# First and last branch product of the merges: high and low halves of u side by side in 512 columns

## The chip, the cores and the metric

The kernel runs on one core of one Trainium2 chip. The metric is the time of one execution on the device, in microseconds (us), as the median of three runs. Everything is fp32 in and out. A profiled execution of the kernel before, recorded by the hardware profiler, is what all rows below come from.

Engines are named as the profile names them: PE is TensorE's matmuls, PEld its weight loads, DVE is VectorE, ACT is ScalarE, POOL is GpSimd, SP is SyncE (it issues the weight DMAs).

## The reference

A transformer of two ordinary layers (attention or retention, then an MLP) followed by one "hybrid" layer, over 256 tokens and a model width of 1024. The change lies in the last step but one of the hybrid layer. Cut to that:

```
ya = (moba_attention(...)  * silu(mg)) @ w_up_moba     # 256x512 @ 512x1024
yb = (dsa_attention(...)   * silu(dg)) @ w_up_dsa
yc = (cross_attention(...) * silu(xg)) @ w_up_cross
gates = sigmoid(glog + b_merge)                        # glog = h @ w_in, 3 x 1024 columns
u = gates[0] * ya + gates[1] * yb + gates[2] * yc
out = rmsnorm(x + u @ w_out)
```

So there are three merges i = 0, 1, 2 (moba, dsa, cross), and each adds gate times branch product into u.

## The kernel before, in words

Every product is made to fp32 precision out of three fp32r products. A weight is split into a high and a low part (`whi` by ACT at L1047, `wlo` = raw - whi by DVE at L1558), and so is the activation; high x high, high x low and low x high are added in PSUM. Weights arrive in halves of 128x1024 elements, numbered in one long order. ACT splits up to 5 halves ahead of the half in use, DVE 4.

A product with transposed output (128 output features by 256 tokens) can be laid out in two ways:

- **Narrow**, `t_half`: three matmuls of 256 columns for each 128 rows of depth (L445, L446, L447). Two output blocks share one PSUM bank of 512 columns, and the result is complete in PSUM. DVE's one `scalar_tensor_tensor` (L2151) reads it there.
- **Wide**, `u_block`: the high and the low activation stand side by side as 512 columns. One matmul of 512 columns multiplies them by the high weight (L521), and one of 256 columns adds the low weight times the high activation to the left half (L530). Each output block takes a whole bank, whose halves have to be added afterwards: ACT copies the right half to SBUF (`branch_low`, L1232), DVE adds the left half to it (L2140), and only then the `scalar_tensor_tensor` runs, from SBUF (L2147).

Each merge i works in two groups g = 0, 1 of 512 features, so a product is named (i, g). A group is six steps on PE: four halves of gate weights "gl" (wide everywhere, `t_block`, L500 and L509), then two halves of the branch's weights "wu". Before the change the products (0, 1), (1, 0), (1, 1) and (2, 0) are wide and (0, 0) and (2, 1) are narrow. Each engine has its own program with the same steps in the same order; between the steps of merge 0 lies the attention "D" (transposes at L680, their evacuation by ACT at L1151 and by DVE at L1705), so that DVE's and ACT's programs reach a step when their own queues get there.

PSUM has eight banks, handed out by a ring in the PE program:

```
b = ring.popleft()                  # take
if b in held:
    w.wait_ge(*at("free", held[b])) # PE waits until the last user's result is read
...
ring.append(bank_of[name])          # give, at the end of the product
```

A bank is thus reused eight takes later or so, and the wait is on whatever instruction frees the product that had it: for a narrow branch product the L2151 that reads it, for a wide one the L2140 that reads that block. Only the *first* instruction of a new product waits, but everything behind it on PE waits too, since an engine runs its instructions in order.

After the last product, (2, 1), PE multiplies u by w_out ("w2o", L572), eight halves of weights. The first four need u of group 0 only. The last four are one piece: `t = [weights(...) for x in range(4)]` waits for all four weight halves, and for u of group 1, before its first matmul. On DVE the order there is: splits of earlier halves, `branch(2, 1)`, `u_low(1)` (L2207; it follows ACT's `u_high(1)`, L1516), then the low parts of w2o's halves 3 to 7 (L1558).

Of the kernel before, what the change touches and what calls it, by code (L numbers as in the profile page):

```python
# [50 lines left out]
XK, XV = 17408, 18432  # L51
EO, ED, EB = 16656, 16784, 17040
SP = 257
WIDE_UP = ((0, 1), (1, 0), (1, 1), (2, 0))
WIDE = ((0, 0), (0, 1), (1, 0), (1, 1), (2, 0), (2, 1))


# [94 lines left out]
def program(nc, A, out):  # L152
    with ExitStack() as st:
# [28 lines left out]
        def up(sem, *events):  # L182

            count[sem] = count.get(sem, 0) + 1
            for name in events:
                value[name] = (S[sem], count[sem])
            return S[sem], 1

        def at(*event):

            return value[event] if rehearsed else value.get(event, (None, 0))
# [24 lines left out]
        def bank(*name):  # L216
            return psum[bank_of.get(name, 0)][:, :]
# [142 lines left out]
        def x_split(stage, k):  # L360

            return ("xl", stage, k)
# [60 lines left out]
        def pe_program(e):  # L423
# [49 lines left out]
            def t_half(label, j, n, nk, xT, splits):  # L473

                i = first_half[label] + j
                h, l = weights(i)
                for c in range(n // 256):
                    m = j * (n // 256) + c
                    if m % 2 == 0:
                        take("mm", label, m // 2)  # L480
                    o = bank("mm", label, m // 2)[:, (m % 2) * 256:(m % 2) * 256 + 256]
                    for k in range(nk):
                        w.wait_ge(*at(*splits(k)))
                        mm = mm3(o, (h[:, k, c * 128:c * 128 + 128], l[:, k, c * 128:c * 128 + 128]),
                                 (xT[0][:, k, :], xT[1][:, k, :]), k == 0, k == nk - 1)
                    if m % 2:
                        mm.then_inc(*up("mm", ("mm", label, m // 2), ("wd", i)))
                        give("mm", label, m // 2)
                    elif c == n // 256 - 1:
                        mm.then_inc(*up("wd", ("wd", i)))  # L490
# [477 lines left out]
            def merge_half(i, s):  # L968
# [5 lines left out]
                elif r < 4:  # L974
                    t_half(("gl", i, g, r // 2), r % 2, 256, 8, hT, lambda k: x_split("sec", k))
                elif (i, g) in WIDE_UP:
                    label, j = ("wu", i, g), r - 4
# [50 lines left out]
        def act_program(e):  # L1028
# [21 lines left out]
            def used(label, j):  # L1050
                weights_to(first_half[label] + j + HI_AHEAD)
# [174 lines left out]
            def branch_low(i, g):  # L1226

                for m in range(4):
                    w.wait_ge(*at("mm", ("wu", i, g), m))
                    if (i, g) != WIDE_UP[0]:  # L1230
                        w.wait_ge(*at("ub", *WIDE_UP[WIDE_UP.index((i, g)) - 1], m // 2))
                    e.activation(UL[:, m, :], bank("mm", ("wu", i, g), m)[:, 256:512], ACT.Copy).then_inc(*up("aev", ("uc", i, g, m)))  # L1232
# [205 lines left out]
            def merge_half(i, s):  # L1438
# [6 lines left out]
                else:  # L1445
                    if r == 2:
                        gate(i, g, 0)
                    if r == 4:
                        gate(i, g, 1)
                if s == 6 and (i, 0) in WIDE_UP:  # L1450
                    branch_low(i, 0)
                used(("gl", i, g, r // 2) if r < 4 else ("wu", i, g), r % 2)
                if s == 11 and (i, 1) in WIDE_UP:
                    branch_low(i, 1)
# [10 lines left out]
            def gate(i, g, c):  # L1465
                w.wait_ge(*at("tt", i, g, c))
                for m in range(2):
                    k = 4 * g + 2 * c + m
                    d = tT[:, 2 * c + m, :]
                    w.wait_ge(*at("hb"))  # L1470
                    a = e.activation(d, d, ACT.Tanh, bias=hb[:, 8 * i + k:8 * i + k + 1], scale=0.5)
                a.then_inc(*up("aev", ("th", i, g, c)))
# [65 lines left out]
        def dve_program(e):  # L1538
# [597 lines left out]
            def branch(i, g):  # L2136
                wide = (i, g) in WIDE_UP
                for m in range(4 if wide else 0):
                    w.wait_ge(*at("uc", i, g, m))
                    e.tensor_tensor(UL[:, m, :], bank("mm", ("wu", i, g), m)[:, 0:256], UL[:, m, :], ALU.add).then_inc(  # L2140
                        *up("dev", ("ua", i, g, m), ("free", ("mm", ("wu", i, g), m))))
                for n in range(2):
                    t, d = tT[:, 2 * n:2 * n + 2, :], uT[:, 4 * g + 2 * n:4 * g + 2 * n + 2, :]
                    w.wait_ge(*at("th", i, g, 1))
                    if wide:
                        w.wait_ge(*at("ua", i, g, 2 * n + 1))
                        x = e.scalar_tensor_tensor(t if i else d, t, 1.0, UL[:, 2 * n:2 * n + 2, :], ALU.add, ALU.mult)  # L2147
                        x.then_inc(*up("dev", ("ub", i, g, n), ("u", i, g)))
                    else:
                        w.wait_ge(*at("mm", ("wu", i, g), n))  # L2150
                        x = e.scalar_tensor_tensor(t if i else d, t, 1.0, two(bank("mm", ("wu", i, g), n)), ALU.add, ALU.mult)  # L2151
                        x.then_inc(*up("dev", ("ub", i, g, n), ("u", i, g), ("free", ("mm", ("wu", i, g), n))))
                    if i:
                        w.wait_ge(*at("ub", i, g, n))
                        e.tensor_tensor(d, d, t, ALU.add).then_inc(*up("dst", ("u", i, g)))
# [307 lines left out]
```

## Time and profile before

| | |
|---|---|
| median of 3 runs | 972.54 us (971.98 to 972.82) |
| the profiled execution | 971.9 us |
| its span in the trace | 970.1 us |
| PE busy | 962.4 us, 99% of the span |
| DVE busy | 705.1 us, 73% |
| ACT busy | 554.9 us, 57% |
| weight and input DMA | 174.72 MB, 180 GB/s on average |

Times in rows are microseconds from the start of the span. A busy PE is one on which a matmul is in flight; matmuls overlap in the records, so the distance between two starts, and not the duration of one, is what a matmul costs in a stream.

### The profile page before, as it was taken

How to read it: one execution, taken by the hardware profiler on the slowest of the kernel's cores; microseconds unless marked ns; L12 is line 12 of the kernel's file. 1: busy time of each engine (PE TensorE's matmuls, PEld its weight loads, DVE VectorE, ACT ScalarE, POOL GpSimd, SP SyncE). 2: the span in 40 equal slices, each digit the busy share in tenths (PEclk: the TensorE clock that was granted, in tenths of full speed). 3: DMA queues.
4: the chain of work that ended last, by engine and by line, in shares of the span. 5: the costliest groups of instructions: out<-in, count | busy, mean ns of one | idle time of the engine just before them, and what ended most of it. 6: DMA issues, size and time to landing. Idle time of an engine off the chain costs nothing.

```text
span 970.1 us, 13894 instructions
## 1 busy us (share of the span) xinstructions
PE 962.4 (99%) x5288; PEld 825.5 (85%) x5288; DVE 705.1 (73%) x1093; ACT 554.9 (57%) x957; POOL 154.3 (16%) x189
## 2 busy tenths in 40 slices
PE   9999999999999999999999999999999999999997
PEld 8888888888888888888888888888888888988885
DVE  6888676766666767786667556666758989888884
ACT  6688655445556553455456444544535857866662
POOL 2741018920001002220001000000550110000000
PEclk9999999999999999999999999999999999999999
DMA  9984535565564664345555665555544563553631
GB/s 343 304 246 169 175 130 193 191 222 176 177 206 149 214 210 133 130 141 204 177 171 184 206 211 180 174 192 182 206 152 150 152 196 112 170 155 131 216 131 44
DMA packets 110338, 174.72 MB, mean 180 GB/s; under 512 B 4288, under 2 KB 73024, under 8 KB 110272
## 3 DMA queue, kind: packets, MB, share of 16 engines
q1 hardware_dynamic: 109840, 173.40, 54.1%
q8 instruction: 42, 0.69, 0.3%
q10 hardware_dynamic: 432, 0.44, 0.1%
q14 instruction: 24, 0.20, 0.1%
HBM read 172.78 MB, written 1.05 MB: 179 GB/s over the span
## 4 chain that ended last, share of the span: by engine, by line
PE 99%; issue 1%; DVE 0%; POOLq 0%; POOL 0%; DVEq 0%
PE ps L572 24%; PE ps L542 14%; PE ps L445 9%; PE ps L447 9%; PE ps L446 9%; PE ps L500 9%; PE ps L546 7%; PE ps L509 5%; PE ps L521 2%; PE ps L668 1%; PE ps L680 1%; PE ps L700 1%; PE ps L530 1%; PE ps L624 1%; PE ps L772 0%
## 5 line engine op out<-in xcount | busy, mean ns | idle before, releaser
L1558 DVE TENSOR_TENSOR wlo<-raw,whi 128x1024 fp32r<-128x1024 f32 x312 | 374.2, 1238 | 13.7 <-PE ps L572 8.3
L1047 ACT ACTIVATE whi<-raw 128x1024 fp32r<-128x1024 f32 x312 | 315.8, 1049 | 34.4 <-PE ps L572 22.0
L572 PE MATMUL ps<-whi,ur 128*128 128x512 f32 x656 | 182.0, 390 | 0.0
L572 PEld LDWEIGHTS ps<-whi,ur 128*128 128x128 f32 x656 | 121.1, 188 | 23.5
L542 PE MATMUL ps<-hT,whi 128*128 128x512 f32 x592 | 140.5, 389 | 0.0
L542 PEld LDWEIGHTS ps<-hT,whi 128*128 128x128 f32 x592 | 110.7, 188 | 22.8
L445 PE MATMUL ps<-whi,hT 128*128 128x512 f32 (+1 forms) x312 | 122.0, 391 | 0.0
L447 PE MATMUL ps<-whi,hT 128*128 128x512 f32 (+1 forms) x312 | 120.0, 385 | 0.0
L446 PE MATMUL ps<-wlo,hT 128*128 128x512 f32 (+1 forms) x312 | 119.9, 384 | 0.0
L1928 DVE TENSOR_TENSOR arena<-ps,arena 128x256 f32<-128x256 f32 x80 | 33.4, 423 | 98.6 <-ACT arena L1290 98.6
L1290 ACT ACTIVATE arena<-ps 128x256 f32<-128x256 f32 x80 | 30.1, 384 | 127.3 <-PE ps L546 127.3
L572 PE MATMUL ps<-wlo,ur 128*128 128x512 f32 x328 | 101.5, 390 | 0.0
L500 PE MATMUL ps<-hT,whi 128*128 128x512 f32 x368 | 97.8, 396 | 0.0
L546 PEld LDWEIGHTS ps<-hT,wlo 128*128 128x128 f32 x592 | 75.9, 191 | 2.9
L546 PE MATMUL ps<-hT,wlo 128*128 128x256 f32 x592 | 76.8, 283 | 0.0
L500 PEld LDWEIGHTS ps<-hT,whi 128*128 128x128 f32 x368 | 66.0, 189 | 12.1 <-issue 0.8
L572 PEld LDWEIGHTS ps<-wlo,ur 128*128 128x128 f32 x328 | 61.6, 188 | 13.2
L447 PEld LDWEIGHTS ps<-whi,hT 128*128 128x128 f32 x312 | 58.6, 188 | 11.8
L445 PEld LDWEIGHTS ps<-whi,hT 128*128 128x128 f32 x312 | 58.7, 188 | 11.6 <-issue 1.0
L446 PEld LDWEIGHTS ps<-wlo,hT 128*128 128x128 f32 x312 | 58.7, 188 | 10.6
L2250 POOL TENSOR_SCALAR stat<-stat 128x1 f32<-128x1 f32 x10 | 1.9, 191 | 335.0 <-ACT arena L1056 334.9
L509 PEld LDWEIGHTS ps<-hT,wlo 128*128 128x128 f32 x368 | 50.9, 190 | 4.2
(232 smaller groups left out, 1284.0 us busy)
## 6 DMA issues: line engine op xcount, KB each, us to landing
raw<-in_w SPq DMA_DIRECT2D x64, 1024.0 KB, 5.6
raw<-in_w_in SPq DMA_DIRECT2D x34, 1024.0 KB, 5.2
raw<-in_w_in_o SPq DMA_DIRECT2D x24, 1024.0 KB, 5.2
raw<-in_w_out_o SPq DMA_DIRECT2D x8, 1024.0 KB, 4.9
raw<-in_w_in_e SPq DMA_DIRECT2D x5, 1024.0 KB, 12.6
raw<-in_w_mem SPq DMA_DIRECT2D x4, 1024.0 KB, 10.2
raw<-in_w_out_e SPq DMA_DIRECT2D x4, 1024.0 KB, 5.0
raw<-in_w_out SPq DMA_DIRECT2D x4, 1024.0 KB, 5.0
```

Source lines behind the costliest of these rows:

```text
L445: e.matmul(o, a[0], b[0], start=start, stop=False)
L446: e.matmul(o, a[0], b[1], start=False, stop=False)
L447: return e.matmul(o, a[1], b[0], start=False, stop=stop)
L500: return e.matmul(o, h[:, k, :], hTs[:, k * 512:k * 512 + 512], start=k == 0, stop=k == 7)
L509: e.matmul(o[:, 0:256], l[:, k, :], hT[0][:, k, :], start=False, stop=False)
L542: e.matmul(o[m], hl[m][0][:, k, :], hTs[:, k * 512:k * 512 + 512], start=k == 0, stop=False)
L546: mm = e.matmul(o[m][:, 0:256], hl[m][1][:, k, :], hT[0][:, k, :], start=False, stop=k == 7)
L572: mm = e.matmul(bank("acc", stage, 2 * tb + i), x[p], t[p % 2][:, 0, 512 * i:512 * i + 512], start=start and p == 0, stop=stop and p == 2)
L1047: e.activation(split_half(i)[0], raw_half(i), ACT.Copy).then_inc(*up("hi", ("hi", i)))
L1290: e.activation(dst, bank("mm", label, m)[:, 256:512], ACT.Copy).then_inc(*up("aev", ("lc", label, m)))
L1558: e.tensor_tensor(l, raw_half(i), h.bitcast(F32), ALU.subtract).then_inc(*up("lo", ("lo", i)))
L1928: e.tensor_tensor(d, bank("mm", label, m)[:, 0:256], d, ALU.add).then_inc(*up("dev", ("t", label, m), ("free", ("mm", label, m))))
```

## The change

The tuple that says which branch products are wide gets (0, 0) and (2, 1) as well, so that all six are.

```diff
-WIDE_UP = ((0, 1), (1, 0), (1, 1), (2, 0))
+WIDE_UP = ((0, 0), (0, 1), (1, 0), (1, 1), (2, 0), (2, 1))
```

Three programs read it. On PE, `merge_half` calls `u_block` instead of `t_half`:

```python
elif (i, g) in WIDE_UP:
    label, j = ("wu", i, g), r - 4
    for c in range(2):
        u_block(label, first_half[label] + j, 2 * j + c, c, 4, ...)
else:
    t_half(("wu", i, g), r - 4, 512, 4, ur[i % 2], ...)
```

On ACT, `branch_low(0, 0)` and `branch_low(2, 1)` are added; on DVE, `branch` adds halves first and reads SBUF after.

TensorE's program around product (0, 0), from its second half of weights to the start of gate product gl (0, 1). Before (L445 to L447 are the narrow product, L680 the transposes of attention D, L500 the gate product's first matmuls):

```order
2448 L445 MATMUL ps<-ur,whi 128x256
2449 L446 MATMUL ps<-ur,whi 128x256
2450 L447 MATMUL ps<-ur,wlo 128x256
2451 L680 MATMUL ps<-cst,arena 128x128 [waits s_aev]
2452 L680 MATMUL ps<-cst,arena 128x128 x3
2453 L680 MATMUL ps<-cst,arena 128x128 [waits s_aev]
2454 L680 MATMUL ps<-cst,arena 128x128 x3
2455 L500 MATMUL ps<-hT,whi 128x512 [waits s_hi,s_dev]
```

The same place after the change; s_dev is the semaphore that DVE raises when it has read a bank:

```order
2415 L521 MATMUL ps<-ur,whi 128x512 x4
2416 L530 MATMUL ps<-ur,wlo 128x256 x4
2417 L521 MATMUL ps<-ur,whi 128x512
2418 L680 MATMUL ps<-cst,arena 128x128 [waits s_aev,s_dev]
2419 L680 MATMUL ps<-cst,arena 128x128 x3
2420 L680 MATMUL ps<-cst,arena 128x128 [waits s_aev,s_dev]
2421 L680 MATMUL ps<-cst,arena 128x128 x3
2422 L500 MATMUL ps<-hT,whi 128x512 [waits s_hi,s_dev]
```

The row L500 waits for s_dev in both, but for another instruction. The ring's takes, one after the other, were before: wu (0,0) bank 0 of 2; two for transposes D; wu (0,0) bank 1 of 2; two for transposes D; gl (0,1). The gate product then got the bank of the gate product gl (0,0) block 2, which L2123 frees. Now the takes are: wu (0,0) blocks 0 and 1; two for transposes; blocks 2 and 3; two for transposes; gl (0,1). That is eight takes after block 0 of wu (0,0), so the gate product gets its bank, which the first L2140 of `branch(0, 0)` frees.

VectorE's program around `branch(0, 0)` (L1705 is the evacuation of the last transposes D, L2123 that of gate product gl (0, 1)):

```order
 L1705 COPY arena<-ps 128x512
-L2151 SCALAR_TENSOR_TENSOR arena<-arena,ps 128x512 x2
+L2140 TENSOR_TENSOR arena<-ps,arena 128x256 x4
+L2147 SCALAR_TENSOR_TENSOR arena<-arena 128x512 x2
 L1558 TENSOR_TENSOR wlo<-raw,whi 128x1024 x2
 L2123 TENSOR_TENSOR arena<-ps,arena 128x256 x2
```

Nothing is moved; four additions are put in front of the two instructions that read the product, and those read SBUF.

VectorE's program around `branch(2, 1)`, in front of w2o's last splits:

```order
 L1558 TENSOR_TENSOR wlo<-raw,whi 128x1024 x2
-L2151 SCALAR_TENSOR_TENSOR arena<-arena,ps 128x512
-L2155 TENSOR_TENSOR arena<-arena 128x512
-L2151 SCALAR_TENSOR_TENSOR arena<-arena,ps 128x512
+L2140 TENSOR_TENSOR arena<-ps,arena 128x256 x4
+L2147 SCALAR_TENSOR_TENSOR arena<-arena 128x512
+L2155 TENSOR_TENSOR arena<-arena 128x512
+L2147 SCALAR_TENSOR_TENSOR arena<-arena 128x512
 L2155 TENSOR_TENSOR arena<-arena 128x512
 L2207 SCALAR_TENSOR_TENSOR ur<-arena,ur 128x512 x2
```

Here the four additions stand ahead of both pairs; before, the first pair stood ahead of the product's end.

## Rows read from the trace of the kernel before

**Rows 1.** The page, part 1: busy time, share, instructions of each engine.

```profile
PE 962.4 (99%) x5288; PEld 825.5 (85%) x5288; DVE 705.1 (73%) x1093; ACT 554.9 (57%) x957; POOL 154.3 (16%) x189
```

**Rows 2.** Waits of TensorE, whole span: all there is (total, times, longest).

```profile
PE ps L772 <- DVE arena L1868: 1.2, 1, 1.2
```

**Rows 3.** Timeline, PE, narrow product (2, 1): start, us, instruction, shapes, count.

```profile
935.88 0.28 PE L445 MATMUL ps<-ur,whi 128*128 128x256 f32 x1
...
941.52 0.28 PE L447 MATMUL ps<-ur,wlo 128*128 128x256 f32 x1
941.64 0.63 PE L572 MATMUL ps<-whi,ur 128*128 128x512 f32 x2
```

**Rows 4.** Timeline, PE, wide product (2, 0), first and last matmuls, and what follows.

```profile
919.09 0.86 PE L521 MATMUL ps<-ur,whi 128*128 128x512 f32 x3
...
924.47 0.40 PE L521 MATMUL ps<-ur,whi 128*128 128x512 f32 x1
924.71 1.77 PE L500 MATMUL ps<-hT,whi 128*128 128x512 f32 x7
```

**Rows 5.** Timeline, PE, behind product (0, 0): transposes D, then gl (0, 1).

```profile
835.10 1.03 PE L680 MATMUL ps<-cst,arena 128*128 128x128 f32 x8
835.89 1.86 PE L500 MATMUL ps<-hT,whi 128*128 128x512 f32 x7
```

**Rows 6.** Timeline, DVE, up to branch (0, 0); brackets: idle before, and releaser.

```profile
834.00 0.76 DVE L2123 TENSOR_TENSOR arena<-ps,arena 128x256 f32<-128x256 f32 x2 [3.69 <-ACT arena L1462]
...
838.07 1.22 DVE L1558 TENSOR_TENSOR wlo<-raw,whi 128x1024 fp32r<-128x1024 f32 x1
839.20 0.68 DVE L1705 COPY arena<-ps 128x512 f32<-128x512 f32 x1
839.80 1.27 DVE L2151 SCALAR_TENSOR_TENSOR arena<-arena,ps 128x512 f32<-128x512 f32 x2
```

**Rows 7.** Timeline, ACT, where branch_low(0, 0) comes in (between these two).

```profile
837.28 0.57 ACT L1151 ACTIVATE arena<-ps 128x512 f32<-128x512 f32 x1
837.76 1.99 ACT L1047 ACTIVATE whi<-raw 128x1024 fp32r<-128x1024 f32 x2
```

**Rows 8.** The page, part 5: TensorE's weight loads for a gate product (last: idle).

```profile
L500 PEld LDWEIGHTS ps<-hT,whi 128*128 128x128 f32 x368 | 66.0, 189 | 12.1 <-issue 0.8
```

**Rows 9.** Timeline, ACT and DVE behind the wide product (2, 0).

```profile
924.90 0.39 ACT L1232 ACTIVATE arena<-ps 128x256 f32<-128x256 f32 x1 [1.02 <-PE ps L521]
...
925.32 0.42 DVE L2140 TENSOR_TENSOR arena<-ps,arena 128x256 f32<-128x256 f32 x1 [0.98 <-ACT arena L1232]
925.66 0.68 DVE L2147 SCALAR_TENSOR_TENSOR arena<-arena 128x512 f32<-128x512 f32 x1
...
927.71 0.69 DVE L2155 TENSOR_TENSOR arena<-arena 128x512 f32<-128x512 f32 x1
...
928.43 1.16 ACT L1516 ACTIVATE ur<-arena 128x512 fp32r<-128x512 f32 x2 [2.20 <-DVE arena L2155]
```

**Rows 10.** Timeline, ACT and DVE behind the narrow product (2, 1).

```profile
943.28 1.16 ACT L1516 ACTIVATE ur<-arena 128x512 fp32r<-128x512 f32 x2 [3.74 <-DVE arena L2155]
943.95 1.29 DVE L2207 SCALAR_TENSOR_TENSOR ur<-arena,ur 128x512 fp32r<-128x512 f32 x2 [0.70 <-ACT ur L1516]
...
945.16 4.63 DVE L1558 TENSOR_TENSOR wlo<-raw,whi 128x1024 fp32r<-128x1024 f32 x4
...
950.10 1.23 DVE L1558 TENSOR_TENSOR wlo<-raw,whi 128x1024 fp32r<-128x1024 f32 x1 [0.31 <-PE ps L572]
```

**Rows 11.** Timeline, PE: inside w2o's last piece, and the last matmul.

```profile
953.00 0.62 PE L572 MATMUL ps<-wlo,ur 128*128 128x512 f32 x2
...
963.20 0.39 PE L572 MATMUL ps<-whi,ur 128*128 128x512 f32 x1
```

**Rows 12.** Windows: length; PE, PEld, DVE, ACT, POOL busy (count); granted clock, DMA.

```profile
968.20:968.60 0.40, 0.00 (x0) 0.00 (x0) 0.00 (x0) 0.00 (x0) 0.00 (x0) 0.82 1.02 389
```

## Prediction, written before the changed kernel ran

> **What bounds the kernel now.** I read the page first: PE has a matmul in flight in 962.4 of 970.1 us [rows 1]. The waits of TensorE say the same more sharply: in the whole span it waited once, for 1.2 us, at the very start [rows 2]. So TensorE is the bound from end to end, and two things follow. Whatever makes its stream shorter shows in the time at once. And whatever makes it wait, for even one microsecond, shows in the time too, and can't be made good later, since there is no later wait that could shrink; after the last matmul only the normalisation and the output follow, some 6.5 us from 963.59 to 970.1, which the change doesn't touch. The questions are what the wide form saves on TensorE, and whether the longer evacuation makes it wait.
>
> **What the wide form saves.** For one branch product TensorE has 48 matmuls of 256 columns before, and 16 of 512 plus 16 of 256 after: 12,288 columns both times. The trace has both forms. The narrow (2, 1) begins at 935.88 and the next work begins at 941.64: 5.76 us [rows 3]. The wide (2, 0) begins at 919.09 and the next begins at 924.71: 5.62 us [rows 4]. So a product gets shorter by 0.14 us, both together by 0.28 us. That is 0.03% of the time; what a measurement of this kernel can tell from no change is about 0.2%, or 1.9 us.
>
> **Product (0, 0): a bank that comes free late.** This is the term that decides. Before, gl (0, 1) gets the bank of an old gate product, and it starts at 835.89, right behind the eight transposes of 835.10 [rows 5]; TensorE doesn't wait, because that bank's release is L2123 at 834.00 [rows 6]. After the change the eight takes reach back only to block 0 of wu (0, 0), whose release is the first L2140 of `branch(0, 0)`. That instruction stands where L2151 stands now, and VectorE gets there at 839.80 [rows 6]: it is almost four microseconds behind TensorE here. From 834.00 to 839.80 VectorE has no idle time in the rows (two additions, five more instructions, each starting as the one before ends), so it doesn't arrive earlier. Its delay comes from ACT, whose copies at L1462 ended VectorE's 3.69 us of idling before 834.00 [rows 6]; all of that lies ahead of the change's first new instruction on either engine.
>
> Does the first L2140 wait for something else? It needs ACT's copy of block 0. ACT does `branch_low(0, 0)` between 837.28 + 0.57 = 837.85 and the splits that now start at 837.76 [rows 7]; a copy takes 0.39 us [rows 9], so the first is there by 838.25, before VectorE comes. So the addition runs from 839.80 for 0.42 us [rows 9], to 840.22. A semaphore from VectorE to its reader costs 0.03 us: L2155 at 927.71 for 0.69 ends at 928.40, and ACT's L1516 starts at 928.43 [rows 9]. Then the gate product's first weight load, 0.19 us [rows 8], which no longer lies under a matmul. It starts at 840.22 + 0.03 + 0.19 = 840.44 instead of 835.89: **+4.55 us**. The 0.14 us of the shorter product is swallowed by this wait, since its end is set by VectorE.
>
> Bounds: the weight load could be done ahead of the wait (-0.19), so +4.36 from below. From above: if ACT's four copies (up to 4 x 0.39) delayed the first addition too, it would start only at 840.2 or so, +4.95. I take +4.55, since the copy of block 0 is the first of the four.
>
> What is queued behind the waiting matmul: all of TensorE's later work, so the gates (0, 1), the D values, the X attention. VectorE's four additions (0.42 us each, up to 1.7 us with no overlap) and ACT's four copies come on top for these engines, but they fall into a stretch where TensorE is now 4.55 us later than before, so everything that they hand to it is relatively earlier by 2.9 us than it was, and it wasn't late then. Blocks 1, 2 and 3 come free 0.4 us after one another, while gl (0, 1) takes its next banks one gate block (some 2.8 us) apart: no second wait. If that cover weren't there, the additions would cost their 1.7 us.
>
> **Product (2, 1): the splits behind it.** In the frame of the old trace, the wide product starts at 935.88 and its last matmul starts 924.47 - 919.09 = 5.38 us later [rows 4], at 941.26 (narrow: 941.52 [rows 3]). Behind the wide (2, 0) ACT's `u_high` starts 928.43 - 924.47 = 3.96 us after that matmul: copy, addition, twice gate and sum [rows 9]. So here at 945.22, against 943.28 now [rows 10]. From `u_high` to the start of w2o's splits it is 945.16 - 943.28 = 1.88 us [rows 10]: they start at 947.10. Five splits are left. Four take 4.63 us now, one alone 1.23, so they start (4.63 - 1.23)/3 = 1.13 apart [rows 10], and the fifth ends at 947.10 + 4 x 1.13 + 1.23 = 952.85. Now the fifth runs apart from the others, at 950.10 to 951.33, as it waits for TensorE to give back a buffer [rows 10]; by 951.6 that has long happened.
>
> TensorE needs the fifth for its last piece. In w2o, two matmuls precede the first low pair of a part; the last piece's first low pair is at 953.00 [rows 11], so the piece starts at 952.53, and with the product shorter by 0.14 it would be ready at 952.39. Now the splits are done 1.2 us ahead of it; then they are 0.46 us late. With 0.03 and 0.19 us as above it starts at 953.07: **+0.54 us** against 952.53, the 0.14 us already in it. The fourth half needed by TensorE, low part at 948.33, is in time for 949.67 (a half takes (952.53 - 941.64)/4 = 2.72 us). Bounds: -0.14 if VectorE were half a microsecond quicker, +0.94 if the five splits didn't overlap at all (5 x 1.23 = 6.15 us in place of 5.75).
>
> **Sum.** 4.55 + 0.54 = +5.09 us. On the profiled execution, 971.9 us with a span of 970.1, that gives 977.0 and a span of 975.2. The median of the runs shown is 0.64 us above that execution, so 972.54 + 5.09 = **977.6 us**, 0.5% slower.
>
> **Rivals.**
>
> *The clock falls in the gap.* TensorE will be without a matmul from about 836.0 (835.10 + 1.03 - 0.14) to 840.44: 4.4 us. At the end of the run its last matmul starts at 963.20 for 0.39 us [rows 11], and the granted clock, full so far, has a mean of 0.82 between 968.20 and 968.60 [rows 12]. From full to half, that puts the fall at 968.46, 4.87 us after the last matmul. Our gap is shorter by 0.4 us, and one fall says little of how much the delay varies. If it falls, the matmuls behind the gap run at 1.2 instead of 2.4 GHz for a time that no row shows; as long as the fall took, 4.9 us, would cost half of that, 2.4 us; a price of nothing is the other end. Time: 978 to 980, middle 979. The Trainium skill, "TensorE: Matmul & The Clock Gate", section "HAM oscillation — how this bites in real kernels", speaks more strongly against the change: by its rule a gap of this length is already enough, and what follows starts cold. By that rule this rival would be the forecast, with 979; the row has the clock hold 4.87 us once, and I go by the row, with 16 in 100 for the fall.
>
> *No wait at the bank (the other side).* If VectorE's first addition ended by 835.7, gl (0, 1) would find its bank free. Then only the tail is left: 972.54 - 0.14 + 0.54 = 972.9; and with the tail hidden too, 972.3. Either isn't slower by what can be told. It decides from 4.5 us earlier on VectorE, and it has no idle time to give between 834.00 and 839.80. What speaks for it is only that the wait is worked out from the order of takes and no row shows it. 6 in 100.
>
> *More waits than these two.* The ring is shifted for the rest of the program, and other products get other banks. If one more release is late by a microsecond or two, it is 979 to 980. Against it: VectorE gains 2.9 us on TensorE from the first wait on. 7 in 100.
>
> *As worked out*: 71 in 100, with a range of its own of 976.9 to 978.5.
>
> **How the numbers follow.** The predicted time is that of the likeliest case. The range leaves out the 6 in 100 without a wait, and of the falls of the clock and the extra waits the dearest; below, it takes in both lower bounds (4.36 - 0.14 = +4.2, so 976.8) and a little less. 976.6 to 980.0. Faster by over 0.2% needs a gain of 1.9 us, for which nothing stands in the profile: 2 in 100. Within 0.2%: 5. Slower: 93.
>
> **What the changed kernel's profile would show.** The waits of TensorE: a line with L500 released by DVE L2140, once, 4.2 to 4.7 us, and a second with L572 released by DVE L1558, 0.3 to 1 us. Both wide products last 5.6 us. VectorE's first L2140 of (0, 0) starts at 839.8, and the granted clock is 1.00 behind the gap. The span is 975.2. Wrong it would be if gl (0, 1) started at 835.8 (the ring was misread), if the first L2140 came clearly before or after 839.8 (its place in the queue was), or if matmuls behind the gap stood 0.46 us apart instead of 0.23 (the clock).

## The result, and the profile after

The changed kernel takes 979.42 us (median of five runs, 978.68 to 979.88) against 972.76 (971.98 to 972.91) for the kernel before: a ratio of 1.0072, with a 95% interval of 1.0061 to 1.0083. It is 0.7% slower. The prediction said slower, 977.6 us, with a range of 976.6 to 980.0; the time is 1.8 us above its likeliest case and where its first rival stood. It lies in the stated range, but above the range of 976.9 to 978.5 that the prediction gave to the likeliest case itself: the stated range holds it only because that range took the rival in.

TensorE's waits in the changed kernel, the whole list (total, times, longest), in place of the one line of [rows 2]:

```profile
PE ps L500 <- DVE arena L2140: 4.3, 1, 4.3
PE ps L772 <- DVE arena L1868: 1.2, 1, 1.2
PE ps L572 <- DVE wlo L1558: 0.5, 1, 0.5
```

Both forecast waits are there, with the forecast releasers and sizes, and no third. The timeline of TensorE around them (start, us, instruction, count, idle before and releaser), which answers to [rows 3], [rows 5] and [rows 11]:

```profile
835.20 0.40 PE L521 MATMUL ps<-ur,whi 128*128 128x512 f32 x1
835.44 1.04 PE L680 MATMUL ps<-cst,arena 128*128 128x128 f32 x8
840.76 3.36 PE L500 MATMUL ps<-hT,whi 128*128 128x512 f32 x7 [4.29 <-DVE arena L2140]
843.91 1.91 PE L509 MATMUL ps<-hT,wlo 128*128 128x256 f32 x8
845.63 2.23 PE L500 MATMUL ps<-hT,whi 128*128 128x512 f32 x8
...
848.64 0.39 PE L500 MATMUL ps<-hT,whi 128*128 128x512 f32 x1
...
943.20 0.86 PE L521 MATMUL ps<-ur,whi 128*128 128x512 f32 x3
...
948.82 0.62 PE L572 MATMUL ps<-whi,ur 128*128 128x512 f32 x2
...
960.33 0.70 PE L572 MATMUL ps<-whi,ur 128*128 128x512 f32 x2 [0.45 <-DVE wlo L1558]
...
971.10 0.39 PE L572 MATMUL ps<-whi,ur 128*128 128x512 f32 x1
```

Look at the widths: seven matmuls L500 take 3.36 us here; in [rows 5] they took 1.86. What follows the gap runs slower than it should. VectorE's timeline at the same place, against [rows 6]:

```profile
834.49 0.76 DVE L2123 TENSOR_TENSOR arena<-ps,arena 128x256 f32<-128x256 f32 x2 [3.69 <-ACT arena L1462]
...
839.70 0.68 DVE L1705 COPY arena<-ps 128x512 f32<-128x512 f32 x1
840.30 1.40 DVE L2140 TENSOR_TENSOR arena<-ps,arena 128x256 f32<-128x256 f32 x4
841.62 1.28 DVE L2147 SCALAR_TENSOR_TENSOR arena<-arena 128x512 f32<-128x512 f32 x2
```

Everything stands as before, shifted by 0.50 us: L2123 from 834.00 to 834.49, the first new addition at 840.30 where L2151 stood at 839.80. The shift is older than the change. It is there in the first tens of microseconds, where both kernels have the same program (the first matmul of L668 starts at 37.5 us before and at 38.0 after), and the profiles of the experiments below have shifts from -0.1 to 0.8 us ahead of the place of their change; it is chance, and I take it out below.

The reason for the width is in the windows (length; PE, PEld, DVE, ACT, POOL busy with counts; the granted clock is the number behind POOL's count):

```profile
838.00:839.00 1.00, 0.00 (x0) 0.00 (x0) 1.00 (x3) 1.00 (x4) 0.00 (x0) 1.00 0.65 123
839.00:840.00 1.00, 0.00 (x0) 0.00 (x0) 1.00 (x2) 1.00 (x3) 0.00 (x0) 0.64 1.00 337
840.00:841.00 1.00, 0.24 (x1) 0.24 (x2) 1.00 (x4) 1.00 (x2) 0.00 (x0) 0.50 1.09 389
...
845.00:846.00 1.00, 1.00 (x5) 0.96 (x5) 0.17 (x1) 0.00 (x0) 0.00 (x0) 0.50 0.77 129
846.00:850.00 4.00, 4.00 (x36) 3.41 (x36) 0.91 (x3) 1.31 (x3) 0.00 (x0) 0.99 0.69 236
```

The clock fell to half while TensorE stood still. A mean of 0.64 in the second window puts the fall at 839.28. The last transposes ended at 835.44 + 1.04 = 836.48, so it came 2.8 us into the gap. It rose again at 846.0 to 846.1, after TensorE had worked 5.3 us at 1.2 instead of 2.4 GHz. All five runs have a mean granted clock of 0.995 or 0.996; those of the kernel before, in the groups below, have 0.998 or 0.999.

### The profile page after: what moved, and what is told of

The parts are those of the page before. It is cut to its first block, busy times and chain, and to the rows that moved or that the text cites. A ratio compares the mean times of both kernels' runs of the same rounds, so it can differ in the third digit from the quotient of the medians.

```text
span 978.0 us, 13851 instructions
## 1 busy us (share of the span) xinstructions
PE 965.6 (99%) x5256; PEld 826.2 (84%) x5256; DVE 708.0 (72%) x1101; ACT 557.1 (57%) x965; POOL 154.8 (16%) x189
## 4 chain that ended last, share of the span: by engine, by line
PE 94%; DVE 3%; ACT 2%; issue 1%; POOLq 0%; POOL 0%; DVEq 0%
PE ps L572 23%; PE ps L542 14%; PE ps L445 9%; PE ps L447 9%; PE ps L446 9%; PE ps L500 7%; PE ps L546 7%; PE ps L509 4%; PE ps L521 3%; PE ps L530 1%; PE ps L700 1%; PE ps L668 1%; PE ps L680 1%; DVE wlo L1558 1%; PE ps L624 1%
## 5 line engine op out<-in xcount | busy, mean ns | idle before, releaser
L1558 DVE TENSOR_TENSOR wlo<-raw,whi 128x1024 fp32r<-128x1024 f32 x312 | 374.0, 1238 | 13.4 <-PE ps L572 8.0
L572 PE MATMUL ps<-whi,ur 128*128 128x512 f32 x656 | 182.4, 391 | 0.5 <-DVE wlo L1558 0.5
L572 PEld LDWEIGHTS ps<-whi,ur 128*128 128x128 f32 x656 | 121.1, 188 | 24.2 <-issue 0.8
L445 PE MATMUL ps<-whi,hT 128*128 128x512 f32 (+1 forms) x312 | 122.2, 392 | 0.0
L447 PE MATMUL ps<-whi,hT 128*128 128x512 f32 (+1 forms) x312 | 120.2, 385 | 0.0
L500 PE MATMUL ps<-hT,whi 128*128 128x512 f32 x368 | 99.6, 402 | 4.3 <-DVE arena L2140 4.3
L572 PE MATMUL ps<-wlo,ur 128*128 128x512 f32 x328 | 101.7, 390 | 0.0
L500 PEld LDWEIGHTS ps<-hT,whi 128*128 128x128 f32 x368 | 67.3, 192 | 16.9 <-DVE arena L2140 4.5
L572 PEld LDWEIGHTS ps<-wlo,ur 128*128 128x128 f32 x328 | 61.6, 188 | 13.1
L445 PEld LDWEIGHTS ps<-whi,hT 128*128 128x128 f32 x312 | 58.8, 188 | 11.8 <-issue 1.0
L447 PEld LDWEIGHTS ps<-whi,hT 128*128 128x128 f32 x312 | 58.7, 188 | 11.8
```

The source lines that it names most:

```text
L445: e.matmul(o, a[0], b[0], start=start, stop=False)
L447: return e.matmul(o, a[1], b[0], start=False, stop=stop)
L500: return e.matmul(o, h[:, k, :], hTs[:, k * 512:k * 512 + 512], start=k == 0, stop=k == 7)
L572: mm = e.matmul(bank("acc", stage, 2 * tb + i), x[p], t[p % 2][:, 0, 512 * i:512 * i + 512], start=start and p == 0, stop=stop and p == 2)
L1558: e.tensor_tensor(l, raw_half(i), h.bitcast(F32), ALU.subtract).then_inc(*up("lo", ("lo", i)))
```

## The experiments

Runs of one group shared the runs of the kernel before: 972.12 us for the first four, 972.2 for the last three.

**Only (0, 0) wide.**

```diff
-WIDE_UP = ((0, 1), (1, 0), (1, 1), (2, 0))
+WIDE_UP = ((0, 0), (0, 1), (1, 0), (1, 1), (2, 0))
```

> Only product (0, 0) is made wide. Theory (the bank of wu (0, 0) block 0 comes free late, and the clock falls in the gap): one wait of L500 for DVE L2140 of 4.2 to 4.4 us, a half clock of some 5 us behind it, no wait at w2o; 4.4 + 2.4 - 0.14 gives 6.3 to 6.8 us over the kernel before, 979.2 or so. Rival (the loss is at the end of the program, or comes from both products together): 973 to 975 us.

Measured: 978.98 us (978.44 to 979.73), ratio 1.0070 (1.0056 to 1.0084). So this one product makes up the loss. The timeline of TensorE shows the wait and the slow matmuls behind it, and nothing at w2o:

```profile
835.59 1.04 PE L680 MATMUL ps<-cst,arena 128*128 128x128 f32 x8
840.93 3.35 PE L500 MATMUL ps<-hT,whi 128*128 128x512 f32 x7 [4.30 <-DVE arena L2140]
...
849.09 0.39 PE L500 MATMUL ps<-hT,whi 128*128 128x512 f32 x1
```

The windows give the fall: a mean of 0.54 puts it at 840.08, 3.45 us after the transposes ended (836.63).

```profile
839.00:840.00 1.00, 0.00 (x0) 0.00 (x0) 1.00 (x2) 1.00 (x4) 0.00 (x0) 1.00 0.91 298
840.00:841.00 1.00, 0.07 (x1) 0.07 (x1) 1.00 (x3) 1.00 (x2) 0.00 (x0) 0.54 1.08 385
```

**Only (2, 1) wide.**

```diff
-WIDE_UP = ((0, 1), (1, 0), (1, 1), (2, 0))
+WIDE_UP = ((0, 1), (1, 0), (1, 1), (2, 0), (2, 1))
```

> Only product (2, 1) is made wide. Theory: a wait of L572 for DVE L1558 of 0.4 to 0.5 us, no other, the clock full; +0.5 us, 973.3. Rival (the tail carries a larger share of the loss than its wait shows, since the end of the kernel hangs on VectorE): +1.5 us or more.

Measured: 972.98 us (11 runs), ratio 1.0007 (0.9999 to 1.0016). In TensorE's waits the line L572 for L1558 is there with 0.5 us, and the one of L500 is not:

```profile
PE ps L772 <- DVE arena L1868: 1.2, 1, 1.2
PE ps L572 <- DVE wlo L1558: 0.5, 1, 0.5
```

The median is 0.86 us above that of the kernel before, where 0.5 was expected; the interval holds both, and no change too. It does not exclude the rival's 1.5 us either: that would be a ratio of 1.0015, just inside. The trace decides. The product starts 0.78 us later than before (936.66 against 935.88), which is the chance shift, and the last matmul 1.37 us later (964.57 against 963.20): the tail costs 0.59 us, and the rival's 1.5 is not there.

**Other banks for the gate product.** The two blocks of gl (0, 1, 0) take the banks of two transposes, D 5 and D 4; the computation stays the same.

```diff
-                b = ring.popleft()
+                other = {("mm", ("gl", 0, 1, 0), 0): ("pt", "D", 5), ("mm", ("gl", 0, 1, 0), 1): ("pt", "D", 4)}.get(name)
+                if other:
+                    b = bank_of[other]
+                    ring.remove(b)
+                else:
+                    b = ring.popleft()
```

> Both products wide, but the two blocks of gl (0, 1, 0) take the banks of the transposes D 5 and D 4, which are free by 835.9 and 838.7, in place of the ring's next two. Nothing else differs from the changed kernel, and VectorE and ACT have the same four additions and copies more. Theory (it is the bank alone): no wait at (0, 0), full clock, only the tail's 0.5 us; 973.1. Rival 1 (the added work of VectorE and ACT costs by itself, bank or not): a wait elsewhere in the merges, 974.5 or more. Rival 2 (the wait only moves to the next bank that is late): one of L500 or L700 for DVE L2140, 1 to 3 us.

Measured: 972.5 us (11 runs, 972.24 to 973.09), ratio 1.0004 (0.9995 to 1.0013). VectorE and ACT do all that they do in the changed kernel. Its timelines, PE and then DVE (the edit puts all lines 5 further down, so L505 is L500 and L2145 is L2140):

```profile
835.67 1.04 PE L685 MATMUL ps<-cst,arena 128*128 128x128 f32 x8
836.46 1.85 PE L505 MATMUL ps<-hT,whi 128*128 128x512 f32 x7
...
840.53 1.41 DVE L2145 TENSOR_TENSOR arena<-ps,arena 128x256 f32<-128x256 f32 x4
```

The gate product now follows the transposes at once, four microseconds ahead of the additions, and its seven matmuls take 1.85 us again. The two banks came free in time, but not by much: ACT has read D 5 at 836.17, 0.3 us before the first block starts, and VectorE D 4 at 838.88, some 0.4 us before the second. So it is the bank alone: the additions and copies cost nothing that can be measured once nobody waits for them. Of the changed kernel's 6.7 us over the kernel before, 0.4 are left.

**The gap filled.** The wait stays, but 18 matmuls whose result nobody reads go ahead of it.

```diff
+                if (i, s) == (0, 6):
+                    w.wait_ge(*at("free", ("pt", "D", 5)))
+                    for _ in range(18):
+                        e.matmul(bank("pt", "D", 5), hTs[:, 0:128], hTs[:, 0:512], start=True, stop=True)
                 if r < 4 and (i, g) in WIDE:
                     take("mm", ("gl", i, g, r // 2), r % 2)
```

> Both products wide, and the wait for the bank as in the changed kernel, but 18 matmuls of 512 columns, whose result nobody reads, go ahead of it into a bank that is free (18 x 0.23 = 4.1 us in a gap of 4.3). Theory (the wait costs 4.4 us and the clock's fall another 2.4): clock 1.00 throughout, gl (0, 1) starts as late as in the changed kernel, and the time is 2.4 us below it, 977.0. Rival (the slow matmuls behind the gap have another cause than idle time, such as contention with the additions on PSUM): 979.4 as the changed kernel.

Measured: 977.0 us (976.85 to 977.31), ratio 1.0050 (1.0036 to 1.0063); a mean granted clock of 0.998 in all four runs. Its timeline of TensorE (the unread matmuls are L974):

```profile
835.66 4.34 PE L974 MATMUL ps<-hT 128*128 128x512 f32 x18
840.19 1.88 PE L500 MATMUL ps<-hT,whi 128*128 128x512 f32 x7 [0.19 <-DVE arena L2144]
...
845.65 0.39 PE L500 MATMUL ps<-hT,whi 128*128 128x512 f32 x1
```

The gate product starts as late as in the changed kernel (840.19 against 840.76, with the transposes at 834.87 against 835.44), but TensorE is busy meanwhile. From its first matmul to the last of its second block it now takes 845.65 - 840.19 = 5.46 us, in the changed kernel 848.64 - 840.76 = 7.88. The difference, 2.42 us, is the price of the slow clock in this pair of traces. The two parts of the loss are told apart: 4.9 us (977.0 - 972.12) are the waits, and some 2.4 the clock. The medians give the clock's part less sharply: 979.42 - 977.0 is 2.4, but each against the runs of the kernel before in its own group, 6.66 and 4.88 us, it is 1.8.

**The gap half and a third filled.** The same edit with 9 and with 5 unread matmuls.

> Both products wide and the ring as in the changed kernel, with 9 unread matmuls ahead of the wait: the idle gap is some 2.3 us instead of 4.3, the gate product starts at the same time. If a shorter gap is enough for the clock to fall: clock 0.5 behind it and 979.4. If not (which the row at the end of the run before, 4.87 us, and the 2.8 and 3.4 us seen in two gaps let expect): 977.0.

> As the one before with 5 unread matmuls: an idle gap of some 3.3 us. The falls seen came 2.8 and 3.4 us after the last work, so this gap lies among them: 977.0 if the clock holds, 977.5 to 979.4 if it falls late in the gap, and runs may differ.

| unread matmuls | idle before gl (0, 1), us | median, us | clock behind the gap in the profile |
|---|---|---|---|
| 18 | 0.19 | 977.0 (976.85 to 977.31) | 1.00 |
| 9 | 2.24 | 977.29 (976.78 to 978.74) | 1.00 |
| 5 | 3.16 | 978.67 (978.37 to 979.03) | 0.50 |
| none, only (0, 0) wide, so without the wait at w2o | 4.30 | 978.98 (978.44 to 979.73) | 0.50 |
| none, the changed kernel | 4.29 | 979.42 (978.68 to 979.88) | 0.50 |

The kernel with 5, timeline of TensorE and windows:

```profile
836.36 1.39 PE L974 MATMUL ps<-hT 128*128 128x512 f32 x5
840.91 3.35 PE L500 MATMUL ps<-hT,whi 128*128 128x512 f32 x7 [3.16 <-DVE arena L2144]
...
847.87 0.39 PE L500 MATMUL ps<-hT,whi 128*128 128x512 f32 x1
```

```profile
840.00:841.00 1.00, 0.09 (x1) 0.09 (x1) 1.00 (x3) 1.00 (x2) 0.00 (x0) 0.89 1.08 386
841.00:842.00 1.00, 1.00 (x3) 0.81 (x4) 1.00 (x4) 1.00 (x3) 0.00 (x0) 0.50 0.76 266
...
844.00:845.00 1.00, 1.00 (x9) 0.93 (x8) 1.00 (x2) 0.00 (x0) 0.00 (x0) 0.90 0.00 0
```

The clock fell at 840.78, 3.0 us after the last unread matmul, when the wait was almost over, and the two gate blocks took 6.96 us, 1.5 more than at full clock. Its four runs all show a mean clock of 0.997. With 9, three runs show 0.998 or 0.999; the remaining one took 978.74 us with 0.997, which looks like a fall even in a gap of 2.2 us, but no profile of that run exists.

**The split moved ahead.** On top of the other banks, VectorE splits w2o's half 3 ahead of `branch(2, 1)`.

```diff
                 if s == 11:
+                    if i == 2:
+                        weights_to(first_half["w2o", 1] + 2)
                     branch(i, 1)
```

> Both products wide, the two other banks for gl (0, 1, 0), and VectorE splits w2o's half 3 ahead of branch (2, 1) instead of behind it. Behind the product four splits are left instead of five, 1.13 us less, and they were 0.5 us late. Theory: TensorE waits nowhere after its first matmul; 0.6 us below the kernel with the other banks alone, and 0.3 below the kernel before, which is less than the comparison can tell: 971.8. Rival (the split ahead only moves the delay into the additions, whose last one waits for ACT anyway): the wait of L572 stays at 0.3 us or more, 972.3.

Measured: 972.0 us (11 runs, 971.47 to 973.05), ratio 0.9997 (0.9988 to 1.0006). The waits of TensorE:

```profile
PE ps L777 <- DVE arena L1873: 1.2, 1, 1.2
PE ps L764 <- ACT hT L1249: 0.7, 1, 0.7
```

The wait of w2o is gone; both lines left lie in the first six microseconds of the program, which the change doesn't touch (the second is one of the chance delays at the start). So the wait at w2o came from the place of the split in VectorE's order, not from the work. This version has both products wide and waits nowhere after its start, and it is as fast as the kernel before within what can be measured: the 0.28 us that the wide form gives are below it. The trace shows them: product (0, 0) starts at 828.97 against 828.90 in the kernel before, 0.07 us later, and the last matmul at 962.97 against 963.20, 0.23 us earlier, so TensorE's stream is 0.30 us shorter between them.

## Why the prediction came out as it did

**The saving: right.** The wide (2, 1) takes 948.82 - 943.20 = 5.62 us, as [rows 4] said; 0.14 us less than narrow. The trace of the kernel without waits has a stream 0.30 us shorter, where 0.28 was forecast for both products.

**The wait at the bank: right in place, releaser and size.** Forecast +4.55 us for the start of gl (0, 1). It moved from 835.89 [rows 5] to 840.76, of which 0.48 us is the shift of the whole trace at that place: +4.39. VectorE's queue was read rightly: the first addition starts on time. (The prediction counted five instructions between L2123 and L2151; the old trace has seven, without idle time between them, so the place stands.) Too dear was the step from the addition to the matmul: the sum had 0.42 + 0.03 + 0.19 = 0.64 us, and it took 840.76 - 840.30 = 0.46, so the 0.19 for a weight load did not come on top. That is close to the prediction's lower bound of 4.36. The releaser is the first L2140, and the kernel with other banks shows that it is the bank and not the added work. The order of takes in the code, held against the two engines' places in the old trace, was enough to find a wait that no row of the old trace had.

**The wait at w2o: right, a little dear.** Forecast was that the last piece comes 0.68 us later behind the product than before (0.54 with the shorter product in it). Its start lies 960.33 - 948.82 = 11.51 us behind the first w2o matmul, against 952.53 - 941.64 = 10.89: +0.62. Up to the last matmul it is 971.10 - 948.82 = 22.28 against 963.20 - 941.64 = 21.56, so +0.72: the piece itself took 0.10 us longer, for which no row gives a cause.

**The clock: the step that failed.** The prediction said: "Our gap is shorter by 0.4 us, and one fall says little of how much the delay varies", and gave the fall 16 in 100. The single row [rows 12], 4.87 us after the last matmul, was taken for the time that the clock holds. In the gaps measured here it fell after 2.8, 3.45 and 3.0 us, so a gap of 4.3 us was well beyond. The rival with the fall, "middle 979", describes the measured 979.4. The Trainium skill, "TensorE: Matmul & The Clock Gate", section "HAM oscillation — how this bites in real kernels", had the rule by which a gap of this length is enough; the trace of the changed kernel agrees with it (0.50 behind a gap of 4.29 us), and so does the mean clock of all its five runs. It would have been the better guide.

The row at the end of the kernel before was one draw of something that varies much. The same delay, from the end of the last matmul to the fall, can be read at the end of every trace here. Shown are the last matmul and a window of the kernel with 18 unread matmuls, then of the one with only (0, 0) wide:

```profile
968.11 0.39 PE L572 MATMUL ps<-whi,ur 128*128 128x512 f32 x1
970.00:971.00 1.00, 0.00 (x0) 0.00 (x0) 0.30 (x3) 0.00 (x1) 0.55 (x1) 0.79 0.00 0
```

```profile
970.97 0.39 PE L572 MATMUL ps<-whi,ur 128*128 128x512 f32 x1
976.00:977.00 1.00, 0.00 (x0) 0.00 (x0) 0.00 (x0) 0.00 (x0) 0.00 (x0) 0.80 0.86 322
```

The means put the falls at 970.58 and 976.60, 2.1 and 5.2 us after the last matmul. In the other traces it is 3.2 us three times, 4.3 in the changed kernel, and 4.9, 5.0 and 5.1. So 4.87 was among the long ones, and it could bound no gap. What sets the delay stays open.

The price of the fall was bounded at 0 to 2.4 us, with the time at half clock guessed at 4.9 us. It was 5.3 us, and 2.42, at the upper end; in the kernel with only (0, 0) wide it was 6.0 us at half clock and 8.16 - 5.46 = 2.70, above the bound.

**The sum.** In the profiled executions, which differ by 979.8 - 971.9 = 7.9 us: 0.48 from the start of the program, 4.39 at the bank, 2.42 by the clock, -0.14 for the shorter (2, 1), 0.62 at w2o. That makes 7.77. Of the 0.13 left, 0.10 is the longer last piece, and 0.03 comes from pricing the clock by the filled kernel's 5.46 us, where the kernel before took 841.32 - 835.89 = 5.43. The medians differ by less, 6.66 us. The start's 0.48 explains a part; the profiled execution of the kernel before was also faster than its five other runs (971.9 against 971.98 to 972.91), and that of the changed kernel slower than its median (979.81 against 979.42). Whether the clock's price differs between runs no trace shows. Without the clock's part the forecast of +5.09 stands against 977.0 - 972.12 = 4.9 in the kernel with the gap filled.

**No more waits; nothing made good later.** Both hold: the list of waits has no other line, and the gate product's delay arrives at the end in full.

## What to carry to other kernels

A product that takes more banks of a ring also changes which release every later product waits for. So for each take around the edit, look up whose bank it gets, find where the releasing engine stands in the old trace at that time, and compare it with the place of the taker; here the two were over four microseconds apart, for a saving of 0.14. If the wide form is wanted all the same, a bank that comes free before it is needed takes the wait and the clock's fall away; of 6.7 us, 0.4 were left. And a wait of TensorE of three microseconds or more, as here, is to be priced with the slow matmuls behind it, which made it half as dear again. One fall of the clock, seen at the end of a program, is no bound for how long a gap may be.

## What the runs showed of the hardware

The delay from TensorE's last work to the fall of the granted clock was not one number: 2.8, 3.0 and 3.45 us in three gaps, and 2.1 to 5.2 us at the ends of the nine traces, 4.87 of them in the kernel before [rows 11, 12]. A gap of 2.24 us left the clock at 1.00 in its profile; the fall after 2.1 us shows that this is not safe ground. After a gap the clock stayed at 0.50 for 3.3 to 6.0 us of matmuls without a pause (840.91 to 844.20 with 5 unread matmuls, 840.93 to 846.90 with only (0, 0) wide), and these cost 1.5 to 2.7 us: 6.96, 7.88 and 8.16 us for two gate blocks that take 5.46. 18 unread matmuls in the gap kept the clock at 1.00 in the profile and made the kernel faster by 2.4 us by the medians (979.42 to 977.0), by 1.8 with each measured against its own runs of the kernel before; the gate product started no later for them.
